# Gates and output projections with tokens as the stationary operand, one chain for four group roots, and 1 MB more of expert weights loaded ahead

## The reference

```python
hn = rms_norm(h, norm_mix)
z, xbc, dt_raw, q_a, kv_a, gate_logits = split(hn @ w_in)
y_ssd = ssd_branch(z, xbc, dt_raw, ...) @ w_ssd_out        # 2048 -> 1024
y_mla = mla_branch(q_a, kv_a, ...) @ w_o                    # 1024 -> 1024
g_ssd, g_mla = split(sigmoid(gate_logits))                  # 2 x 1024
h = h + (g_ssd * y_ssd + g_mla * y_mla) @ w_out
h = h + moe_ffn(rms_norm(h, norm_ffn), ...)                 # top 4 of 32 experts
return rms_norm(h, norm_final)[:, 16:]
```

## Time and profile before

| | us |
|---|---|
| median of 3 runs | 1300.4 |
| the profiled execution, its own time | 1299.7 |
| its span, first to last instruction | 1297.8 |
| TensorE busy in the span | 98% |
| granted TensorE clock, mean | 0.996 |
| HBM read | 465 MB, mean 359 GB/s |

### The profile page before, as it was taken

The page is one execution under the profiler, slowest core; times in us unless marked ns, Lnnn a source line. Parts: engine busy times, 40 slices in busy tenths (PEclk is TensorE's granted clock), DMA queues, the critical chain, the costliest instruction groups (busy, mean ns, idle before and its releaser), DMA issues.

```text
span 1297.8 us, 17445 instructions
## 1 busy us (share of the span) xinstructions
PE 1271.6 (98%) x7011; PEld 638.8 (49%) x7011; DVE 467.1 (36%) x1088; ACT 347.1 (27%) x671; POOL 28.6 (2%) x46
## 2 busy tenths in 40 slices
PE   9999999999999999999999999999999999999997
PEld 6889999999873333333333333333333333333332
DVE  5978889887852112111121111112111112111112
ACT  4767788653441010110110110010110011010102
POOL 1000000022010000000000000000000000000000
PEclk9999999999999999999999999999999999999999
DMA  8332356457889999999999999999999999999996
GB/s 314 123 147 115 101 226 224 167 195 287 324 323 422 424 405 428 428 428 429 432 431 431 432 426 430 433 431 433 431 429 427 430 434 431 430 431 431 424 429 284
DMA packets 32179, 467.23 MB, mean 360 GB/s; under 512 B 4112, under 2 KB 4144, under 8 KB 8704
## 3 DMA queue, kind: packets, MB, share of 16 engines
q1 hardware_dynamic: 31840, 466.00, 86.0%
q10 hardware_dynamic: 288, 0.52, 0.1%
HBM read 465.43 MB, written 1.08 MB: 359 GB/s over the span
## 4 chain that ended last, share of the span: by engine, by line
PE 46%; DMA 23%; DVE 0%; SPq 0%; ACT 0%; issue 0%; DVEq 0%
PE bank L1604 44%; DMA ring<-wts_dram 16%; DMA work<-wts_dram 7%; PE bank L2022 1%; PE bank L2016 1%; PE bank L2046 1%; SPq L442 0%; SPq L576 0%; DVE work L1598 0%; DVE work L1564 0%; ACT work L1013 0%; DVE work L1580 0%; DVE work L1508 0%; DVEq L107 0%; DVE work L1510 0%
## 5 line engine op out<-in xcount | busy, mean ns | idle before, releaser
L1604 PE MATMUL bank<-ring,work 128*64 128x512 f32 (+2 forms) x2168 | 493.3, 589 | 15.3 <-DMA ring<-wts_dram 14.6
L1604 PE MATMUL bank<-work 128*64 128x512 f32 (+8 forms) x2184 | 428.7, 549 | 2.9 <-DVE work L1504 1.0
L1604 PEld LDWEIGHTS bank<-ring,work 128*64 128x64 f32 (+1 forms) x2168 | 157.0, 139 | 302.1 <-issue 266.0
L1604 PEld LDWEIGHTS bank<-work 128*64 128x64 f32 (+3 forms) x2184 | 148.2, 143 | 254.2 <-issue 237.8
L1531 DVE COPY work<-bank 128x256 f32<-128x256 f32 x30 | 12.7, 425 | 447.5 <-PE bank L2046 447.5
L1604 PE MATMUL bank<-hn_hi,split 128*128 128x256 f32 (+1 forms) x896 | 172.3, 288 | 0.2 <-ACT work L721 0.2
L1604 PEld LDWEIGHTS bank<-hn_hi,split 128*128 128x128 f32 x896 | 141.4, 189 | 0.9 <-ACT work L721 0.4
L1604 PE MATMUL bank<-hn_lo,split 128*128 128x256 f32 (+1 forms) x448 | 127.1, 284 | 0.0
L1508 DVE TENSOR_SCALAR work<-bank 128x512 f32<-128x512 f32 x32 | 22.1, 692 | 262.5 <-PE bank L1604 262.5
L1109 DVE TENSOR_TENSOR split<-ring,split 128x1024 fp32r<-128x1024 f32 x88 | 108.9, 1247 | 18.8 <-ACT split L682 18.4
L940 ACT ACTIVATE work<-bank 128x512 f32<-128x512 f32 x31 | 18.5, 597 | 325.6 <-PE bank L1604 325.6
(11 more groups left out here) (302 smaller groups left out, 895.4 us busy)
## 6 DMA issues: line engine op xcount, KB each, us to landing
ring<-wts_dram SPq DMA_DIRECT2D x83, 2048.0 KB, 18.9
ring<-wts_dram SPq DMA_DIRECT2D x20, 4096.0 KB, 30.0
work<-wts_dram SPq DMA_DIRECT2D x20, 4096.0 KB, 30.2
ring<-slabs_dram SPq DMA_DIRECT2D x23, 2048.0 KB, 8.5
work<-wts_dram SPq DMA_DIRECT2D x23, 2048.0 KB, 14.1
ring<-wts_dram SPq DMA_DIRECT2D x7, 1024.0 KB, 17.5
ring<-decay_rows SPq DMA_DIRECT2D x16, 256.0 KB, 3.6
work<-wts_dram SPq DMA_DIRECT2D x4, 1024.0 KB, 11.1
```

The lines of the kernel that those rows point to most:

```text
L1604: return pe.matmul(o, lhsT, rhs, start=start, stop=stop)
```

## The change

- **Gates, wo and so by tokens.** `token_piece` takes the place of `split_mm` and `split_pair_mm` for `g`, `wo` and `so`: 128 tokens stationary, 512 weight columns moving, 12 matmuls of 512 for a piece, two banks (two blocks of tokens) for four or eight pieces. The gates (`gt`), and the mixed result (`mix`) now have tokens on the partitions. The tanh of the gates is 2 instructions of 512 columns per four pieces instead of one of 256 per piece.
- **Transposes.** `mix` is transposed by TensorE before `wout`: `mix_transposes(0)`, 8 transposes of 128 x 128, after the second piece of the second half of `so`; `mix_transposes(1)`, 8 more, after the first piece of `wout`. ScalarE and VectorE read the transposes from PSUM for `mT_hi` and `mT_lo` (`mix_hi_of`, `mix_lo_of`).
- **Merging** on VectorE goes from 8 x 1 and 8 x 5 instructions of 256 columns to 2 x 2 and 2 x 4 of 512, and 4 subtractions of 512.
- **Roots.** One ScalarE square root over all 1024 group columns at u = 5, and on VectorE one `reciprocal` of 1024 columns at u = 6 and one Newton step of three instructions of 1024 at u = 7, 8, 9. The scalings of the four groups stand at u = 10, 12, 14, 16, with `y2_hi` one u later.
- **The queue of loads.** Unit 3 of expert 1 goes to right after the end of `so`; unit 2 of expert 1 is loaded in two halves; and the first half (1 MB) of the second down unit of expert 1 goes over the norm row `nf`, the vectors and the mask, after routing has used them (`late_place`).

The core of the diff (the rest moves tiles to other places, and lets semaphores count otherwise):

```diff
-            def split_pair_mm(o, p, lo_hi, start, stop):
+            def token_piece(p, banks, k0, hi, lo, start, stop):
                 pe.wait_ge(lo_ready, p + 1)
-                ws = split[p % NSPLIT]
-                for k in range(KD):
-                    if k or not start:
-                        mm(o[:, SEQ:2 * SEQ], ws[:, 1, k, :], lo_hi(k)[:, 1, :], False, False)
-                    last = mm(o[:, :], ws[:, 0, k, :], lo_hi(k), start and k == 0, stop and k == KD - 1)
-                    if start and k == 0:
-                        mm(o[:, SEQ:2 * SEQ], ws[:, 1, k, :], lo_hi(k)[:, 1, :], False, False)
+                ws = overlays[f"split{p % NSPLIT}"]
+                for kk in range(2):
+                    w_hi, w_lo = ws[:, kk * 512:(kk + 1) * 512], ws[:, PIECE + kk * 512:PIECE + (kk + 1) * 512]
+                    for b in range(2):
+                        o = bank[banks[b]][:, :]
+                        mm(o, hi(k0 + kk, b), w_hi, start and kk == 0, False)
+                        mm(o, hi(k0 + kk, b), w_lo, False, False)
+                        last = mm(o, lo(k0 + kk, b), w_hi, False, stop and kk == 1)
                 return last
...
+            def mix_transposes(n):
+                for b in range(2):
+                    pe.wait_ge(merged, 4 + 2 * n + b + 1)
+                    for j in range(4):
+                        last = pe.transpose(bank[MIX_BANKS[n][b]][:, j * P:(j + 1) * P], mix[:, n, b, j * P:(j + 1) * P], ident[:, :])
+                    last.then_inc(mix_trans, 1)
...
+            def merge_state(n):
+                d.wait_ge(out_done, KD + 8 * (n + 1))
+                for b in range(2):
+                    d.wait_ge(merged, 4 + 2 * n + b)
+                    link(d.scalar_tensor_tensor(mtmp, gt[:, b, n * 512:(n + 1) * 512], 1.0, bank[HALF_BANKS[n][b]][:, :],
+                                                ALU.add, ALU.mult))
+                    d.tensor_tensor(mix[:, n, b, :], mix[:, n, b, :], mtmp, ALU.add).then_inc(merged, 1)
...
# ScalarE, loop over u; ROOT_AT, CHAIN_AT, SCALE_AT = 5, 6, (10, 12, 14, 16)
+                if u == ROOT_AT:
+                    a.wait_ge(gsum_read, GROUPS)
+                    a.activation(tmp_g, var_g, ACT.Sqrt).then_inc(group_root, 1)
+                if u - 1 in SCALE_AT:
+                    g = SCALE_AT.index(u - 1)
                     a.wait_ge(yn_ready, CHUNKS_PER_GROUP * (g + 1))
...
# VectorE, loop over u
             for u in range(PSO - PG):
                 lo_of(PG + u + 2)
+                if u == CHAIN_AT:
+                    d.wait_ge(group_root, 1)
+                    link(d.reciprocal(rstd_g, tmp_g))
+                elif u == CHAIN_AT + 1:
+                    link(d.tensor_tensor(tmp_g, rstd_g, rstd_g, ALU.mult))
+                elif u == CHAIN_AT + 2:
+                    link(d.scalar_tensor_tensor(tmp_g, var_g, -0.5, tmp_g, ALU.mult, ALU.mult))
+                elif u == CHAIN_AT + 3:
+                    link(d.scalar_tensor_tensor(rstd_g, tmp_g, 1.5, rstd_g, ALU.add, ALU.mult))
+                elif u in SCALE_AT:
+                    g = SCALE_AT.index(u)
+                    for c in range(CHUNKS_PER_GROUP * g, CHUNKS_PER_GROUP * (g + 1)):
+                        d.scalar_tensor_tensor(y2T[:, c, :], y2T[:, c, :], v("ssd_norm", c, 1), rstd_g[:, g * SEQ:(g + 1) * SEQ],
+                                               ALU.mult, ALU.mult).then_inc(yn_ready, 1)
...
# SyncE
-            sp.wait_ge(out_done, 2 * KD)
+            sp.wait_ge(out_done, 3 * KD)
             load_half(1, 0, 1, True)
             load_extra(1)
+            load_w1(1, 3, True)
...
             load_half(0, 1, 0, False)
-            load_w1(1, 3, True)
+            load_half(1, 2, 0, True)
             sp.wait_ge(xn_ready, 4)
+            sp.wait_ge(mask_ready, 2)
+            sp.dma_start(late_place, unit_of(1, W1_UNITS + 1)[:, 0:UNIT // 2]).then_inc(late_in, 16)
             sp.wait_ge(h1_squared, 4)
             sp.wait_ge(h1_kept, 1)
-            load_w1(1, 2, True)
+            load_half(1, 2, 1, True)
...
             sp.wait_ge(down_done, 1)
-            load_w2(1, 1)
+            sp.dma_start(w2_sb[1][:, UNIT // 2:UNIT], unit_of(1, W1_UNITS + 1)[:, UNIT // 2:UNIT]).then_inc(w2_in[1], 16)
```

More of the change, by code:

```diff
@@ L131, in meta_ssd_mla_moe @@
         vec = sb("vec", VEC_COLS)
+        keymask = sb("keymask", L)
         shifted = sb("shifted", 2 * P)
@@ L887, in _, with mix_hi_of @@
                         a.activation(y2_hi[c], y2T[:, c, :], ACT.Copy).then_inc(y2_hi_ready, 1)
[L888 to L889 removed]
+                if u < 16 and u % 4 == 3:
+                    if u == 3:
                         a.wait_ge(proj_read, U["z", NX - 1] + 1)
[L891 to L897 removed]
+                        a.wait_ge(ssdy_read, NX)
+                    a.wait_ge(proj_done, U["g", u] + 1)
+                    i = u // 4
+                    for b in range(2):
+                        a.activation(gt[:, b, i * 512:(i + 1) * 512], bank[HALF_BANKS[i % 2][b]][:, :], ACT.Tanh,
+                                     scale=0.5).then_inc(proj_read, 2)
+            def mix_hi_of(n):
+                for b in range(2):
+                    a.wait_ge(mix_trans, 2 * n + b + 1)
+                    a.activation(mT_hi[n][:, :, b * P:(b + 1) * P],
+                                 bank[MIX_BANKS[n][b]][:, :].rearrange("p (k t) -> p k t", k=4), ACT.Copy).then_inc(mT_hi_ready, 1)
+            for j in range(2 * KD):
+                hi_of(PSO + 2 + j)
+                if j == KD + 2:
+                    mix_hi_of(0)
             def square_half(b, n):
@@ L920, in top_weights @@
                 a.activation(ex[:, b, :], lg[:, b, :], ACT.Exp, bias=nm4[:, b:b + 1]).then_inc(top_exp, 1)
-            for q in range(2, 7):
+            hi_of(POUT + 2)
+            mix_hi_of(1)
+            for q in range(3, 7):
                 hi_of(POUT + q)
@@ L1397, in _ @@
+                if u in (19, 23):
+                    merge_attention(u // 4 - 4)
+            for j in range(2 * KD):
+                lo_of(PSO + 2 + j)
+                if j == KD - 1:
+                    merge_state(0)
+                elif j == KD + 2:
+                    mix_lo_of(0)
+            merge_state(1)
+            lo_of(POUT + 2)
+            mix_lo_of(1)
             d.wait_ge(xres_in, 32)
@@ L1439, in weights @@
                 link(d.tensor_scalar(PW[:, 2 + b, 0:E], ex[:, b, :], r4[:, b:b + 1], None, ALU.mult))
-            for q in range(2, 6):
+            for q in range(3, 6):
                 lo_of(POUT + q)
@@ L1860, in gsum_of, with gate_piece, rows @@
                 mm(bank[7][:, 0:SEQ], ones[:, :], ysq[:, 3, :]).then_inc(gsum_done, 1)
+            def gate_piece(c):
+                i, q = c // 4, c % 4
+                if q == 0 and i == 1:
+                    pe.wait_ge(proj_read, U["z", NX - 1] + 1)
+                elif q == 0 and i:
+                    pe.wait_ge(proj_read, U["g", 0] + 4 * (i - 1))
+                def rows(b):
+                    return slice(NMETA + b * P, NMETA + (b + 1) * P)
+                token_piece(PG + c, HALF_BANKS[i % 2], 2 * q, lambda k, b: hn_hi[:, k, rows(b)], lambda k, b: hn_lo[:, k, rows(b)],
+                            q == 0, q == 3).then_inc(proj_done, 1)
             pe.wait_ge(kT_ready, MH)
@@ L2100, in down @@
                         pe.wait_ge(extra_in[k - 6], 32)
-                    elif k == 4:
+                    elif first == 1 and k == 4:
+                        pe.wait_ge(late_in, 16)
+                    elif k == (6 if first == 1 else 4):
                         pe.wait_ge(w2_in[1], 16 * t if later else 16 * (t + 1))
```

168 lines of the change are left out of this document (70 added, 98 removed).

## The result

| | before | after |
|---|---|---|
| median of 20 runs each, us | 1300.3 | 1301.9 |
| range of the runs, us | 1298.9 to 1301.5 | 1301.4 to 1303.0 |
| the profiled execution, own time / span, us | 1299.7 / 1297.8 | 1301.7 / 1299.6 |
| TensorE enters the experts at, us | 390.65 | 392.48 |
| from there to the end of the span, us | 907.1 | 907.1 |

The ratio is 1.0013, 95% interval 1.0008 to 1.0019. The time lies inside the range that I gave (1296.0 to 1302.8), but the change is a loss that can be told from nothing, where I had forecast 1298.5, a small gain. The forecast's own case ended at 1300.0; the time is in the range only because the range took in most of the rival of eight passes.

A forecast was written before the change was run, and what follows sets the result against it. The weight stream sets the end, tied to TensorE's entry into the experts. Terms -4.9 + 1.8 + 1.0 + 1.0 - 0.8 = -1.9 us gave 1297.8 for the profiled execution, median 1298.5 us; range 1296.0 to 1302.8.

The forecast's parts named there:

- The forecast's own case: Whole kernel: all terms as costed, 1298.5 us, covering 1297.0 to 1300.0; chance 0.42.
- rival of eight passes: Root chain on VectorE: reciprocal takes 8.5 us, stall 4.8 instead of 1.0, time 1302.3 us; chance 0.22.
- Bound, one for one: Entry into the experts: the end moves one for one with the front, plus at most 1.9 us for bytes ahead.
- Part 1, matmuls: g, wo and so: the token form removes 1.9 + 1.3 + 1.7 = 4.9 us, all on TensorE's path.
- Part 2, transposes: so and wout: 16 transposes add 1.8 us on TensorE's path; waits for both merges are covered.
- Part 3, the reciprocal: g stage: a reciprocal of 4.8 to 5.0 us delays g piece 9's low part; +1.0 us, 0 to 4.8.
- My bounds, 1.27 and 8.5 us: Reciprocal of 1024 columns: at least a same-size subtraction, 1.27 us, at most eight passes for each column, 8.5 us.
- The lead, 3.8 us: g stage: nothing is lost up to a reciprocal of 3.8 us; beyond it each us counts.
- the place of the stall: TensorE idle before g piece 9, near 270 us, waiting for its low part behind the reciprocal.
- Part 4, the ladder: Scalings at every second u, with rounding, tanh, high and low parts, stretched by GpSimd's subtractions: +1.0 us, 0 to 2.
- Part 5, the queue: Weight loads of expert 1 moved ahead: -0.8 us, within 0 to -1.9.
- My own first paragraph: Experts: the stream's last wait for buffers freed by TensorE is at about 485 us, tied to the entry.

The follow-up runs named there:

- e11: Changed kernel with the old root chain put back, scalings at u = 4, 10, 16, 22; 1298.0 us, ratio to the kernel before 0.9984.
- e6: Changed kernel with each of the 16 transposes of the mixed result done twice; 1303.7 us, ratio to the kernel before 1.0028.
- e7: Changed kernel with the gates computed from the attention result instead of the normalized input as stationary operand; 1301.0 us, one run.

## Why the prediction was wrong

The new form can be priced without its stalls in e11, stage by stage (before, e11, after; us, from the start of the first matmul of one stage to that of the next):

| stage | before | e11 | after |
|---|---|---|---|
| first g piece to wo | 47.3 | 46.1 | 48.8 |
| wo | 23.0 | 21.8 | 23.2 |
| so, with 8 transposes | 45.2 | 44.4 | 44.4 |
| wout, with 8 transposes, norm, routing | 34.8 | 35.8 | 35.8 |

- **Bound, one for one: right.** The rest is 906.4 to 907.8 us in the table, over entries from 388.1 to 399.9, without a trend.
- **Part 1, matmuls: the size was off.** wo -1.3 and so -1.7 (-0.8 with 0.9 for its transposes) came as costed. g gave -1.3 instead of -1.9: I took wout's 0.68 us for three matmuls, but with the normalized input as stationary operand they take 0.695. That alone would be 1.0 less; some 0.3 came back, as g pieces 1 to 3, with what stands between them, went from 3.25, 3.17 and 2.87 us to 3.16, 2.93 and 2.73. In sum -4.2 instead of -4.9.
- **Part 2, transposes: right.** +0.9 at each place, +1.8, and the second merge was covered.
- **Part 3, the reciprocal: the step that failed.** +2.7 instead of +1.0 (2.56, and 0.1 for the first matmul after it). I drew a slope through 1 and 4 columns, 4.7 ns for each. The forms from 4 to 1024 columns give (1745 - 178) / 252 = 6.2, (3348 - 1745) / 256 = 6.3 and (6547 - 3348) / 512 = 6.2 ns for each. In the two rows of 164 and 178 ns most is the fixed part, and a difference of 14 ns can't carry an extrapolation over 1020 columns. My bounds, 1.27 and 8.5 us, held the value; the slope should not have chosen within them. Eight passes for each column don't hold either: the prediction read them out of the Trainium skill (VectorE: DVE Perf Modes, section First, the fixed hardware budget: a repeat count of 8) and made 8.5 us of them. Measured are 6.25 ns for each column, six times a plain one's 1.02, and 6.55 us for all; the measurement decides. With 6.55 us in my own sum the time would have been 1300.2, no change; what made it a loss are the pace of g, the ladder and the queue, 2.0 us together. The lead, 3.8 us, was right (4.0 measured), and so was the place of the stall.
- **Part 4, the ladder: mechanism right, size near.** +1.5 instead of +1.0: 1.17 of stall and some 0.3 of slower matmuls behind the gaps. I had priced a stretched low part; the scalings stretch as well, four in 2.63 instead of 1.66 us.
- **Part 5, the queue: wrong.** Nothing that a run shows, instead of -0.8 (the times alone leave room for it, the bytes don't). My own first paragraph said that the stream waits for buffers up to 485 us, and I still gave 0.8 for bytes ahead of that place. The bytes ahead were used up 80 us after the entry, at about 472 us.
- **Sum.** -4.2 + 1.8 + 2.7 + 1.5 + 0 = +1.8 us, which is the difference of the two spans. From -1.9 that is 3.7 us: 1.7 from the reciprocal, 0.8 from the queue, 0.7 from the pace of g, 0.5 from the ladder.

## What to carry to other kernels

A chain that feeds another engine through a few rotating buffers has a lead of so many us, here 4.0, and no single instruction on it may be longer; cut long ones, and leave room between them for the lead to come back. Fewer and larger instructions are worth nothing on an engine that isn't the bound, and they can cost what 99 small ones didn't. And bytes loaded ahead count only if no later place makes the stream wait for a buffer: find the last such place first.

## What the runs showed of the hardware

- A VectorE reciprocal of float32 takes 6.25 ns for each column (6.55 us for 1024), about six times a plain subtraction of the same size (1.22 us).
- VectorE's scaling (0.47 us) that meets a GpSimd subtraction takes 0.96 us, and a low part 1.59 instead of 1.22; sixteen such subtractions take 18.1 us in one row beside VectorE's low parts, two of them 1.44 us by themselves.
- A gap of TensorE can cost more than itself: behind 9.0 us idle the granted clock was 0.50 for some 4 us (2.0 us lost), behind 2.4 us idle in the profile of e6 for 2 us and more (1.4 lost) and behind a stall of 2.79 us in that of e7, and in five other profiles with the stall of 2.56 us not at all. What decides it stays open.
- TensorE takes 0.2267 us for a matmul of 512 columns (float32, a new 128 x 128 stationary block each time) out of one tile, and 0.2315 out of another. The offset of 16 columns isn't the cause; whether it is the row length or the place of the tile stays open.
